# Moving modulation chunks of a two-layer transformer from the first layer to the second and changing their order

## The reference

```
c_act = silu(c)
for l in range(DEPTH):                       # DEPTH = 2
    mod = c_act @ ada_w[l] + ada_b[l]        # ada_w[l]: 1024 x 6144
    sh1, sc1, g1 = mod[0:D], mod[D:2D], mod[2D:3D]
    sh2, sc2, g2 = mod[3D:4D], mod[4D:5D], mod[5D:6D]
    h = rmsnorm(x, norm1_g[l]) * (1 + sc1) + sh1
    x = x + g1 * token_mix(h, ...)
    h = rmsnorm(x, norm2_g[l]) * (1 + sc2) + sh2
    x = x + g2 * grouped_moe(h, ...)
return rmsnorm(x, final_g)
```

## Time and profile before

| | |
|---|---|
| median of 3 runs | 1925.41 us (1923.14 to 1927.06) |
| the profiled execution, its own time | 1920.22 us |
| its span in the trace | 1918.4 us |
| PE busy | 1802.7 us (94% of the span) |
| DVE busy | 926.4 us (48%) |
| ACT busy | 371.9 us (19%) |
| DMA | 465.90 MB, mean 243 GB/s |

### The profile page before, as it was taken

How to read it: one execution, slowest core, us unless ns; L and a number is a source line. 1 busy time by engine, 2 the same in 40 slices (tenths; PEclk the granted TensorE clock), 3 DMA queues, 4 the chain that set the end, 5 groups by cost and what they waited for, 6 DMA issues and landing times.

```text
span 1918.4 us, 46239 instructions
## 1 busy us (share of the span) xinstructions
PE 1802.7 (94%) x21052; PEld 1566.8 (82%) x21052; DVE 926.4 (48%) x1652; ACT 371.9 (19%) x723; POOL 25.1 (1%) x24
## 2 busy tenths in 40 slices
PE   5899987999998999997999998998999989999999
PEld 3678766899997688676899996657888988878899
DVE  4887877200004868765000004685677651233355
ACT  3013242100002022332000013273111110021110
POOL 0000200000000000200000000000000000000000
PEclk8999999999999999998999999999999999999999
DMA  9995447699996682643999994113887543434330
GB/s 359 387 386 201 177 174 310 235 392 423 422 413 220 233 316 82 220 176 140 374 402 423 421 401 161 46 43 104 291 302 264 208 171 132 159 122 158 131 111 24
DMA packets 180604, 465.90 MB, mean 243 GB/s; under 512 B 5152, under 2 KB 55936, under 8 KB 172288
## 3 DMA queue, kind: packets, MB, share of 16 engines
q1 hardware_dynamic: 180192, 463.83, 64.6%
q10 hardware_dynamic: 288, 0.26, 0.0%
HBM read 463.03 MB, written 1.05 MB: 242 GB/s over the span
## 4 chain that ended last, share of the span: by engine, by line
PE 81%; DVE 12%; DMA 3%; ACT 2%; issue 2%; SPq 0%; ACTq 0%; DVEq 0%
PE pair L400 79%; DMA ring<-in_ada_w 3%; DVE AR L1577 2%; DVE XH L1577 2%; PE pair L1046 1%; DVE RST L1639 1%; DVE AR L1823 1%; ACT AR L1292 1%; DVE AR L1833 0%; SPq L291 0%; PE pair L904 0%; DVE AR L1837 0%; DVE XH L1824 0%; DVE AR L1877 0%; DVE AR L1815 0%
## 5 line engine op out<-in xcount | busy, mean ns | idle before, releaser
L400 PE MATMUL pair<-XH,ring 128*128 128x256 f32 (+1 forms) x3328 | 749.5, 386 | 22.4 <-ACT XH L1193 17.2
L400 PEld LDWEIGHTS pair<-XH,ring 128*128 128x128 f32 (+1 forms) x3328 | 628.1, 190 | 133.2 <-issue 39.8
L400 PE MATMUL pair<-AR,ring 128*64 128x88 f32 (+2 forms) x14336 | 696.8, 249 | 15.4 <-issue 9.1
L400 PEld LDWEIGHTS pair<-AR,ring 128*64 128x64 f32 (+1 forms) x14336 | 667.9, 139 | 38.7 <-issue 18.6
L2076 DVE TENSOR_TENSOR AR<-AR,pair 128x352 f32<-128x352 f32 x32 | 16.7, 521 | 397.5 <-PE pair L400 397.5
L1577 DVE SCALAR_TENSOR_TENSOR AR<-ring,CACT,AR 128x512 f32<-128x512 f32 x245 | 184.2, 752 | 8.7
L400 PE MATMUL pair<-AR 128*64 128x128 f32 (+3 forms) x1600 | 132.0, 292 | 10.2 <-ACT AR L1464 3.3
L400 PEld LDWEIGHTS pair<-AR 128*64 128x64 f32 (+3 forms) x1600 | 106.2, 146 | 19.8 <-issue 6.2
L2282 DVE SCALAR_TENSOR_TENSOR AR<-pair,VEC,AR 128x255 f32<-128x255 f32 x88 | 41.9, 476 | 96.3 <-ACT AR L1489 96.3
L1396 ACT ACTIVATE AR<-pair 128x352 f32 (+1 forms) x64 | 26.4, 465 | 300.9 <-PE pair L400 300.9
L1489 ACT ACTIVATE AR<-pair,VEC 128x256 f32<-128x256 f32 x88 | 36.6, 466 | 214.3 <-PE pair L400 214.3
(11 more groups left out here) (270 smaller groups left out, 1110.8 us busy)
## 6 DMA issues: line engine op xcount, KB each, us to landing
ring<-in_ada_w SPq DMA_DIRECT2D x48, 2048.0 KB, 13.8
ring<-in_w_gate SPq DMA_DIRECT2D x32, 2048.0 KB, 11.0
ring<-in_w_up SPq DMA_DIRECT2D x32, 2048.0 KB, 11.0
ring<-in_w_down SPq DMA_DIRECT2D x32, 2048.0 KB, 11.6
ring<-in_ffn_w_up SPq DMA_DIRECT2D x44, 1024.0 KB, 7.6
ring<-in_w_in SPq DMA_DIRECT2D x18, 2048.0 KB, 15.9
ring<-in_ffn_w_down SPq DMA_DIRECT2D x8, 2048.0 KB, 8.0
ring<-in_sc_w_in SPq DMA_DIRECT2D x6, 2048.0 KB, 8.1
```

The lines of the kernel that those rows point to most:

```text
L400: return pe.matmul(o, lhsT, rhs, start=start, stop=stop, **kw)
```

## The change

It edits the table in `plan` and nothing else. In the first layer hq has no job in front of it (two before) and bb has one (two before); 17 jobs are left there, 20 before. In the second layer hi, wo0 and wo1 have two jobs each (one before), 15 altogether, 12 before. The three jobs that change layer are chunks 7, 10 and 11 of block 0, layer 1 (the second half of sh2, and g2). The first layer's list is in another order: chunks 8 and 9 (sc2) come before 4, 5 and 6. So every job behind moves to an earlier or later projection. The two-vector jobs, block 1 layer 0 k = 0..3, stood in front of hq, hi, hg and lat1 of the second layer, and now stand in front of hg, lat1, lat2 and gt0.

```
--- before.py
+++ after.py
@@ -86,16 +86,19 @@
 def plan():
 
     order, before = [("ada", m) for m in FIRST_ADA], {}
-    jobs = [[(0, 0, k) for k in range(4, 12)] + [(0, 1, k) for k in range(12)], [(1, 0, k) for k in range(12)]]
+    early = (0, 1, 2, 3, 8, 9, 4, 5, 6)
+    jobs = [[(0, 0, k) for k in range(4, 12)] + [(0, 1, k) for k in early],
+            [(0, 1, k) for k in (7, 10, 11)] + [(1, 0, k) for k in range(12)]]
+    counts = [(0, 0, 2, 2, 2, 2, 1, 1, 0, 0), (0, 1, 2, 1, 1, 1, 1, 1, 0, 0)]
+    late = dict(bb=1, wo0=2, wo1=2)
     for l in range(DEPTH):
         for n, name in enumerate(PROJ):
-            count = 0 if n in (0, 8, 9) else (2 if l == 0 and n < 6 else 1)
-            before[name, l] = [jobs[l].pop(0) for _ in range(count)]
+            before[name, l] = [jobs[l].pop(0) for _ in range(counts[l][n])]
             order += [("ada", m) for m in before[name, l]] + [(name, l)]
         before["kv", l] = [jobs[l].pop(0) for _ in range(2)]
         order += [("qu", l)] + [("ada", m) for m in before["kv", l]] + [("kv", l), ("ba", l)]
         for name in LATE:
-            before[name, l] = [jobs[l].pop(0) for _ in range(2 - l)]
+            before[name, l] = [jobs[l].pop(0) for _ in range(late[name])]
             order += [("ada", m) for m in before[name, l]] + [(name, l)]
         order += [("moe", l)] + [("", l)] * 47
     order += [("wqkv", k) for k in range(3)] + [("wwo", k) for k in range(2)]
```

## The result

| | before | after |
|---|---|---|
| median | 1925.06 us (1923.14 to 1927.06, 4 runs) | 1942.09 us (1939.29 to 1945.87, 4 runs) |
| profiled execution | 1920.22 us | 1939.51 us |
| its span, mean granted clock | 1918.4 us, 0.982 | 1937.7 us, 0.976 |

The changed kernel takes 1.0093 times as long (95% interval 1.0075 to 1.0111): 17 us more, where 10.1 were predicted. The direction is right; the time is just above the range.

A forecast was written before the change was run, and what follows sets the result against it. The prediction took PE, 81% of the chain, as the bound, with waits for modulation sums on DVE and for transfers. Its gains and losses summed to +10.1 us, from 1925.4 to 1935.5 us, range 1929.5 to 1940.

The forecast's parts named there:

- Part 1: First layer's projections: shorter waits before hi and none before hg, lat1 and lat2, a gain of 6.3 us.
- Part 2: First layer's bb, wo0, wo1: saved sum hidden behind ACT, -0.6 us, and a clock drop after idle PE, +1.0.
- Part 3: Second layer's projections: a loss of 7.7 us, mainly gt0 waiting 6.25 us more for a double sum behind lat2.
- the clock's 2.0: Second layer's gt0: lower granted clock after 5.8 us of idle PE, +2.0 us (0 to 2.5).
- Part 4: Second layer's bb, wo0, wo1: two chunks at wo0 and wo1, +7.3 us, and a clock drop, +1.0; together 8.3.
- my rivals: On clock drops: none, or hi's goes, +4.5 to +7.5 us, chance 0.22; drops everywhere or late transfer, +12 to +15, 0.15.

The follow-up runs named there:

- e2: The changed kernel, unchanged, profiled and timed again: 1939.54 us, ratio 1.0088 to before.
- e5: The changed kernel with 22 never-executed products in the first layer's jumped-over block and 42 in the second's: 1937.37 us, ratio 1.0073 to before.
- e13: The kernel of e11 timed and profiled again: 1937.07 us, ratio 1.0066 to before.
- e3: The changed kernel with the second layer's two-vector chunks one place forward and a one-vector chunk at gt0: 1934.49 us, ratio 1.0052 to before.
- e8: The changed kernel with one chunk instead of two at the second layer's wo0 and a one-vector chunk more at hq: 1934.82 us, ratio 1.0063 to before.
- e1: The kernel before, unchanged, profiled once more: 1923.37 us.
- e6: The kernel before with 43 never-executed products in the first layer's jumped-over block and 21 in the second's: 1930.57 us, ratio 1.0036 to before.
- e9: The kernel before with 64 never-executed products (256 instructions) in the first layer's jumped-over block: 1924.22 us, ratio 0.9995 to before.
- e10: The kernel before with 52 never-executed products in the first layer's jumped-over block and 12 in the second's: 1930.57 us, ratio 1.0034 to before.
- e11: The changed kernel with 10 never-executed products in the first layer's jumped-over block and 54 in the second's: 1938.45 us, ratio 1.0073 to before.

## Why the prediction was right in direction and 7 us short

- *Part 1, -6.3:* right in mechanism. In the first profile hf to gt0 is 85.07 instead of 91.24 us, -6.2; over five profiles against before's mean of 91.4 it is -2.7 to -6.3, -4.6 in the mean (-6.0 in after and e2), because hf, hi or their neighbour runs at a lower clock in some (17.3 us from hi to hg in e5 and e13, 14.5 in after). hi's product began at 73.03, not near 71.5: hf itself began 0.84 us later, and the wait before it is 2.77, not 2.4.
- *Part 2, +0.4:* right. Scores to wo1 stays at 62.6 to 63.1 against 62.7. The freed sum is hidden behind ACT, and the idle time moved from bb to wo0 (4.29 us for 4.7 foreseen, and the 1.82 before the product beside it).
- *Part 3, +7.7:* right. lat2 to gt0 +6.6 for 6.25 (the wait 5.71 for 5.8), gt0 to scores +1 to +3 for the clock's 2.0, hf to lat2 -1.0 for -0.6. e3 undid it for 7 us.
- *Part 4, +8.3:* right, +8.1 to +9.0; e8 shows it to be wo0's second chunk.
- Together the four measure 11.8 us in the means of five (-4.6 + 0.1 - 1.0 + 6.6 + 2.2 + 8.5), and 9.0 us in after and e2, the two profiles without padding (-6.0 + 0.1 - 1.6 + 6.6 + 0.9 + 9.0), for 10.1.
- *The step that failed* is the one that put the rest at nothing: "at both expert stages six chunks are in the ring as before" was taken for the whole condition of those stages. Three chunks less are turned on PE ahead of the first layer's experts, so their code lies elsewhere to the 16 KB pieces: +5.6 us (241.8 to 247.4, means of two profiles of each kernel). The second layer's stage has all 32 chunks ahead of it in both kernels, and is unchanged. The order of both kernels shows the count of products ahead of the jump; the trace of before shows "issue" pauses of 0.4 to 1.2 us one or two pieces apart. I read neither.
- *A second, smaller one* is wo1 to the first expert product in the first layer, +1.7 us. The window view of the stretch from the end of wo1's product to the first expert product, before and then after:

```profile
319.80:347.70 27.90, 17.67 (x77) 13.29 (x76) 18.46 (x62) 9.58 (x16) 0.68 (x1) 0.82 0.27 102
```

```profile
316.30:346.20 29.90, 19.54 (x79) 14.89 (x78) 18.65 (x63) 9.71 (x16) 0.68 (x1) 0.71 0.28 106
```

The mean granted clock is 0.82 and 0.71 (the column behind POOL): more of the stretch at the low level, for about the same work. In the second layer the same stage is 41.7 in before and 43.8 in its repeat e1, again at 0.82 and 0.71, so it flips by itself. It is 43.2 to 43.8 in the first layer of all five profiles of the change, but 41.8 in e8, whose first layer is the same (0.82). So it is no fixed consequence of the change; whether the change makes it likelier is open.

In after and e2 that makes 9.0 + 5.6 + 1.8 = 16.4 us, against 17.0 and 14.5 by the medians of the two measurements (19 with the means of all five; 19.3 between the two first spans). The drops of the clock, the subject of my rivals, moved single terms by 1 to 3 us, in both directions.

## What to carry to other kernels

Work of one engine that is moved behind another's must be priced at the place where it lands: one sum more is free behind a long product and costs its full 6 us behind a short one, and a chunk off a stage that waits for something else (bb) brings nothing. And when instructions move from ahead of a long stage to behind it, and the stage is one that is entered by a jump, look at where its code lies: "issue" pauses in a loop's first pass, one or two pieces apart, are the mark of it, and a few instructions in a block that is never executed are enough to test it.

## What the runs showed of the hardware

- Code that is never executed changed the time by 7 us of 1923 (e6: 172 instructions in the first layer's block), and 256 instructions there, a whole 16 KB piece, changed nothing (e9: 0.9995).
- PE's pauses in the first pass of that code end 1.1 to 1.6 us behind the end of a transfer of instructions (99 pauses of over 0.3 us in 17 profiles).
- Under a stream of weights of 364 to 381 GB/s (360 to 407 us of before, after, e10, e11) a 16 KB piece of instructions came every 4.0 to 7.2 us, against 3.1 to 4.1 us with few weights moving; PE used one up in 5.07 us. Well placed code (before, e11) had a mean of 5.6 us, the changed kernel and e10 6.2 to 6.3: the pace goes with the position, and why is open.
- A loop whose body is some 1540 instructions of PE long (six chunks of 128 records, each with its weight load) was fetched in its first pass only: 12 transfers in 63 us for it and the code ahead of it, then one in 182 us.
